# One 512-column matmul for the high and low halves of the input in the transposed up tiles

## The reference, cut to what matters

```python
D_MODEL = 1024; SEQ = 256; DEPTH = 2; D_FF = 2816; FFN_KERNEL = 3

def conv_ffn(h, w_up, conv_w, conv_b, w_down):
    u = causal_depthwise_conv(h @ w_up, conv_w, conv_b)
    gate, val = u[..., :D_FF], u[..., D_FF:]
    return (jax.nn.gelu(gate, approximate=True) * val) @ w_down
...
        y = conv_ffn(rms_norm(h, ffn_norm_pre[l]), ffn_w_up[l], ffn_conv_w[l], ffn_conv_b[l], ffn_w_down[l])
        h = h + rms_norm(y, ffn_norm_post[l])
```

## Time and profile before

| | us |
|---|---|
| median of 3 runs | 845.71 (845.55 to 846.62) |
| the profiled execution | 845.01 |
| its span, first to last instruction | 843.0 |
| TensorE busy | 820.3 (97% of the span) |
| VectorE busy | 615.0 (73%) |
| ScalarE busy | 498.7 (59%) |

### The profile page before, as it was taken

The page is one execution under the profiler, slowest core; times in us unless marked ns, Lnnn a source line. Parts: engine busy times, 40 slices in busy tenths (PEclk is TensorE's granted clock), DMA queues, the critical chain, the costliest instruction groups (busy, mean ns, idle before and its releaser), DMA issues.

```text
span 843.0 us, 12986 instructions
## 1 busy us (share of the span) xinstructions
PE 820.3 (97%) x5152; PEld 732.6 (87%) x5152; DVE 615.0 (73%) x1080; ACT 498.7 (59%) x765; POOL 28.4 (3%) x53
## 2 busy tenths in 40 slices
PE   3999999999999999999999999999999999999997
PEld 2998898889889999998899889888988899999885
DVE  5689996575675887886577899848567488877653
ACT  4555977565656666564454578656566466666441
POOL 2000000010010000000020000001000000000000
PEclk9999999999999999999999999999999999999999
DMA  9655343574474466557647553455535526565651
GB/s 338 226 175 175 126 148 112 165 237 139 125 248 131 147 200 189 171 190 225 198 143 255 172 156 106 142 173 194 206 112 178 186 89 197 190 200 180 208 187 50
DMA packets 40363, 147.31 MB, mean 175 GB/s; under 512 B 4528, under 2 KB 4656, under 8 KB 40304
## 3 DMA queue, kind: packets, MB, share of 16 engines
q1 hardware_dynamic: 38144, 138.90, 51.1%
q0 software_dynamic: 2160, 7.59, 2.7%
HBM read 145.43 MB, written 1.05 MB: 174 GB/s over the span
## 4 chain that ended last, share of the span: by engine, by line
PE 89%; DVE 5%; ACT 2%; DMA 2%; issue 2%; POOL 0%; SPq 0%; DVEq 0%; POOLq 0%; ACTq 0%
PE acc L1383 7%; PE acc L1385 6%; PE acc L1384 6%; PE acc L1366 4%; PE acc L1368 4%; PE acc L1367 4%; PE acc L1423 4%; PE acc L1425 3%; PE acc L1424 3%; PE psAB L1366 3%; PE psAB L1367 3%; PE psAB L1368 3%; PE psCD L1383 3%; PE psCD L1385 3%; PE psCD L1384 3%; PE psCD L1334 3%
## 5 line engine op out<-in xcount | busy, mean ns | idle before, releaser
L832 DVE TENSOR_TENSOR wlo<-raw,whi 128x1024 fp32r<-128x1024 f32 x240 | 288.1, 1221 | 84.0 <-ACT whi L479 81.7
L479 ACT ACTIVATE whi<-raw 128x1024 fp32r<-128x1024 f32 x240 | 249.8, 1057 | 104.0 <-PE acc L1368 45.3
L1383 PE MATMUL acc<-xT_hi,whi 128*128 128x256 f32 x432 | 123.4, 286 | 1.5 <-DVE wlo L832 1.5
L1384 PE MATMUL acc<-xT_lo,whi 128*128 128x256 f32 x432 | 122.2, 283 | 0.0
L1385 PE MATMUL acc<-xT_hi,wlo 128*128 128x256 f32 x432 | 122.2, 283 | 0.0
L1383 PEld LDWEIGHTS acc<-xT_hi,whi 128*128 128x128 f32 x432 | 82.8, 192 | 4.7 <-issue 2.7
L1384 PEld LDWEIGHTS acc<-xT_lo,whi 128*128 128x128 f32 x432 | 82.8, 192 | 0.2
L1385 PEld LDWEIGHTS acc<-xT_hi,wlo 128*128 128x128 f32 x432 | 82.8, 192 | 0.0
L1383 PE MATMUL psCD<-xT_hi,whi 128*128 128x256 f32 x192 | 54.6, 285 | 0.0
L1385 PE MATMUL psCD<-xT_hi,wlo 128*128 128x256 f32 x192 | 54.3, 283 | 0.0
L1384 PE MATMUL psCD<-xT_lo,whi 128*128 128x256 f32 x192 | 54.3, 283 | 0.0
(11 more groups left out here) (275 smaller groups left out, 2017.4 us busy)
## 6 DMA issues: line engine op xcount, KB each, us to landing
raw<-stream_dram SPq DMA_DIRECT2D x256, 512.0 KB, 4.0
gpre<-gain_dram POOLq DMA_DIRECT2D x7, 512.0 KB, 5.7
gpost<-gain_dram POOLq DMA_DIRECT2D x6, 512.0 KB, 5.4
memn<-mem_dram SPq DMA_DIRECT2D x2, 512.0 KB, 5.9
h<-x_dram SPq DMA_DIRECT2D x1, 1024.0 KB, 12.4
out_dram<-h SPq DMA_DIRECT2D x2, 512.0 KB, 2.6
cst<-const_dram SPq DMA_DIRECT2D x1, 896.0 KB, 16.9
gpre<-gain_dram SPq DMA_DIRECT2D x1, 512.0 KB, 5.3
```

What stands on the lines that cost most here:

```text
L479: act.activation(home(g)[0], raw[:, s * GW:(s + 1) * GW], ACT.Copy).then_inc(w_hi.sem, 1)
L832: dve.tensor_tensor(lo, raw[:, cols], hi.bitcast(F32), ALU.subtract).then_inc(w_lo.sem, 1)
L1383: pe.matmul(dst, whi[:, cols], hi[:, toks], start=k == 0 and c % 2 == 0, stop=False)
L1384: pe.matmul(dst, whi[:, cols], lo[:, toks], start=False, stop=False)
```

## The change

The input's halves become one tensor `xT`, so that `xT_both[:, :, k, :]` is the high and the low half of block k, 512 columns in two pieces. `halves_product` takes the place of `transposed_product` for tiles 2 to 10: for each (k, c) one matmul moves both halves past the `whi` block (512 columns, one PSUM bank: `whi`·hi in its first half, `whi`·lo in its second), and one adds `wlo`·hi (256 columns) to the first half. A chunk so takes a whole bank and a tile 4 banks; two sets of 4 are used in turn, and a tile waits for the sum of the tile two before it.

The two halves of a bank are added outside TensorE. ScalarE copies the second halves to `ffu` (`up_low`, 2 instructions of 512 columns), VectorE adds the first halves to them there (`up_sum`, 2 instructions of 512 columns), and `gate` and `up_taps` of tiles 2 to 10 read `ffu` in SBUF instead of PSUM. In both engines' lists one split stands now between these and `gate` / `up_taps`, and one after.

```diff
-        xT_hi = sb("xT_hi", KC * SEQ, F32R)
-        xT_lo = sb("xT_lo", KC * SEQ, F32R)
+        xT = sb("xT", 2 * KC * SEQ, F32R)
+        xT_hi, xT_lo = xT[:, 0:KC * SEQ], xT[:, KC * SEQ:2 * KC * SEQ]
+        xT_both = xT[:, :].rearrange("p (s k n) -> p s k n", s=2, k=KC)
...
+        ffu = V[:, D:D + 4 * SEQ]
...
-        up_banks = [psAB, accs[1], psCD, accs[0]]
+        up_banks = [psAB, [a[:, :] for a in accs[0]]]
 
         def up_chunk(j, c):
 
-            return up_banks[j % 4][c // 2][:, c % 2 * SEQ:(c % 2 + 1) * SEQ]
+            if j < 2:
+                return up_banks[j][c // 2][:, c % 2 * SEQ:(c % 2 + 1) * SEQ]
+            return ffu[:, c * SEQ:(c + 1) * SEQ]
...
+        def up_pair(j, n):
+
+            return ((psC, acc2[1]) if j % 2 == 0 else (psA, acc2[0]))[n]
...
                     if j >= 2:
-                        act.wait_ge(w_used.sem, w_used.at(l, G_UP + (j + 1) * PER_TILE))
+                        act.wait_ge(u_sum.sem, u_sum.at(l, j - 1))
...
+                def up_low(j):
+
+                    act.wait_ge(w_used.sem, w_used.at(l, G_UP + (j + 1) * PER_TILE))
+                    if j > 2:
+                        act.wait_ge(y_conv.sem, y_conv.at(l, j))
+                    for n in range(2):
+                        act.activation(ffu[:, n * 2 * SEQ:(n + 1) * 2 * SEQ].rearrange("p (c n) -> p c n", c=2),
+                                       up_pair(j, n)[:, :, SEQ:2 * SEQ], ACT.Copy).then_inc(u_lo.sem, 1)
...
                     split(G_UP + (j + 1) * PER_TILE - 1 + AHEAD)
+                    up_low(j)
+                    split(G_UP + (j + 1) * PER_TILE + AHEAD)
                     gate(j)
...
+                def up_sum(j):
+
+                    for n in range(2):
+                        dve.wait_ge(u_lo.sem, u_lo.at(l, 2 * (j - 2) + n + 1))
+                        lo = ffu[:, n * 2 * SEQ:(n + 1) * 2 * SEQ].rearrange("p (c n) -> p c n", c=2)
+                        e = dve.tensor_tensor(lo, up_pair(j, n)[:, :, 0:SEQ], lo, ALU.add)
+                    e.then_inc(u_sum.sem, 1)
...
                     split(G_UP + (j + 1) * PER_TILE - 1 + AHEAD)
+                    up_sum(j)
+                    split(G_UP + (j + 1) * PER_TILE + AHEAD)
                     up_taps(j)
...
+                                both = dst.rearrange("p (s n) -> p s n", s=2)
+                                if k == KC - 1:
+                                    pe.matmul(dst[:, 0:SEQ], wlo[:, cols], xT_both[:, 0, k, :], start=False, stop=False)
+                                    e = pe.matmul(both, whi[:, cols], xT_both[:, :, k, :], start=False, stop=True)
+                                else:
+                                    pe.matmul(both, whi[:, cols], xT_both[:, :, k, :], start=k == 0, stop=False)
+                                    e = pe.matmul(dst[:, 0:SEQ], wlo[:, cols], xT_both[:, 0, k, :], start=False, stop=False)
...
-                transposed_product(G_UP + 2 * PER_TILE + 1, 3, X, up_banks[2], k0=2)
-                for j in range(3, UP_TILES):
-                    if j >= 4:
-                        pe.wait_ge(y_conv.sem, y_conv.at(l, j - 3))
-                    transposed_product(G_UP + j * PER_TILE, PER_TILE, X, up_banks[j % 4])
+                halves_product(2, 1, 3)
+                pe.wait_ge(y_conv.sem, y_conv.at(l, 2))
+                halves_product(3)
+                for j in range(4, UP_TILES):
+                    pe.wait_ge(u_sum.sem, u_sum.at(l, j - 3))
+                    halves_product(j)
```

More of the change, by code:

```diff
@@ L226, in hybrid_trunk @@
         ffg = [V[:, b * 2 * SEQ:(b + 1) * 2 * SEQ] for b in range(2)]
-        def bank(name):
-            return ctx.enter_context(nc.psum_tensor(name, [P, NT], F32))
-        accs = [[bank(f"acc{s}{t}") for t in range(TOK)] for s in range(2)]
+        ffu = V[:, D:D + 4 * SEQ]
+        acc2 = [ctx.enter_context(nc.psum_tensor(f"acc{s}", [P, TOK, NT], F32)) for s in range(2)]
+        accs = [[a[:, t] for t in range(TOK)] for a in acc2]
         psA = ctx.enter_context(nc.psum_tensor("psAB", [P, 2, NT], F32))
@@ L235, in hybrid_trunk, with up_halves @@
         psCD = [psC[:, 0], psC[:, 1]]
-        up_banks = [psAB, accs[1], psCD, accs[0]]
+        up_banks = [psAB, [a[:, :] for a in accs[0]]]
         def up_chunk(j, c):
-            return up_banks[j % 4][c // 2][:, c % 2 * SEQ:(c % 2 + 1) * SEQ]
+            if j < 2:
+                return up_banks[j][c // 2][:, c % 2 * SEQ:(c % 2 + 1) * SEQ]
+            return ffu[:, c * SEQ:(c + 1) * SEQ]
+        def up_halves(j, n):
+            return up_pair(j, n // 2)[:, n % 2]
+        def up_pair(j, n):
+            return ((psC, acc2[1]) if j % 2 == 0 else (psA, acc2[0]))[n]
         attended = accs[1][1][:, 0:SEQ]
@@ L346, in hybrid_trunk @@
         u_tr = signal("u_tr", 2)
+        u_lo = signal("u_lo", 2 * (UP_TILES - 2))
+        u_sum = signal("u_sum", UP_TILES - 2)
         y_tap2 = signal("y_tap2", UP_TILES)
@@ L1386, in transposed_product, with halves_product @@
                                               stop=k == KC - 1 and c % 2 == 1)
+                        e.then_inc(w_used.sem, 1)
+                def halves_product(j, first=0, groups=PER_TILE):
+                    for g in range(G_UP + j * PER_TILE + first, G_UP + j * PER_TILE + first + groups):
+                        s = g % RING
+                        pe.wait_ge(w_lo.sem, w_lo.at(l, g + 1))
+                        for u in range(UNITS):
+                            k = (g - G_UP - j * PER_TILE) * UNITS + u
+                            for c in range(4):
+                                cols = slice(s * GW + u * NT + c * P, s * GW + u * NT + (c + 1) * P)
+                                dst = up_halves(j, c)
+                                both = dst.rearrange("p (s n) -> p s n", s=2)
[5 more added lines that the diff above has]
+                                    e = pe.matmul(dst[:, 0:SEQ], wlo[:, cols], xT_both[:, 0, k, :], start=False, stop=False)
                         e.then_inc(w_used.sem, 1)
@@ L1733, in up_flip @@
                 def up_flip(j):
+                    pe.wait_ge(rows_in.sem, rows_in.at(l, (j + 2) * TOK))
                     for t in range(TOK):
-                        pe.wait_ge(rows_in.sem, rows_in.at(l, (j + 1) * TOK + t + 1))
                         for c in range(4):
@@ L1751, in _ @@
                 up_flip(0)
-                transposed_product(G_UP + 2 * PER_TILE, 1, X, up_banks[2])
+                halves_product(2, 0, 1)
                 up_flip(1)
-                transposed_product(G_UP + 2 * PER_TILE + 1, 3, X, up_banks[2], k0=2)
-                for j in range(3, UP_TILES):
-                    if j >= 4:
-                        pe.wait_ge(y_conv.sem, y_conv.at(l, j - 3))
-                    transposed_product(G_UP + j * PER_TILE, PER_TILE, X, up_banks[j % 4])
+                halves_product(2, 1, 3)
[4 more added lines that the diff above has]
+                    halves_product(j)
                 G = tuple(gT[:, part * 2 * SEQ:] for part in range(2))
                 g_order = [4 * (k // 2) + k % 2 for k in range(FFC)]
-                pe.wait_ge(y_conv.sem, y_conv.at(l, UP_TILES - 2))
+                pe.wait_ge(u_sum.sem, u_sum.at(l, UP_TILES - 3))
                 for g in range(DOWN_GROUPS):
```

## The result

The changed kernel takes 863.44 us in the median (863.01 to 863.60), the kernel before beside it 845.63 (845.39 to 846.62). The ratio is 1.0206, with a 95% interval from 1.0194 to 1.0219: 2.1% slower. The prediction was 863.1.

What follows compares the result with a forecast made beforehand. The VectorE-ScalarE loop of 12.45 us a tile was to replace TensorE as the bound, delaying each layer by 8.7 us: 845.0 + 17.4 = 862.4, plus 0.7 to the median, 863.1 us; range 853 to 870.

Steps and rivals of the forecast that it cites:

- The bound changes: Tiles 2 to 10: the VectorE-ScalarE loop, 12.45 us, replaces TensorE, 11.09 us a tile, as what sets the pace.
- The loop: Waits between VectorE and ScalarE from one tile's taps to the next: 10.62 us before, 12.45 us after the change.
- adds and signal: Loop piece: two VectorE adds of 512 columns, 1.22 us, plus 0.12 us for the signal and ScalarE's start.
- gate until taps: Loop piece from the gate's start on ScalarE to the taps on VectorE: 1.94 us before, 2.11 us after.
- The 0.17 us for a gate that reads SBUF: Extra time for a gate's four ScalarE instructions reading SBUF instead of PSUM; the other bound was 0.
- Start and end: Stage edges: taps of tile 2 at 282.8, tile 10 12.1 us late, seventh down group 8.7 us late per layer.
- The step from the profiled execution to the median: Median of the runs taken as 0.7 us above the profiled execution: 862.4 becomes 863.1.
- The rival of the taps on SBUF: VectorE's taps get faster reading SBUF, 0.065 us each: loop 11.93 us, time 854 us; chance 0.12.
- the wide matmul's pace: TensorE's 512-column matmul in two pieces starts 0.227 us before the next; a pair takes 0.347 us.
- the change's own gain: TensorE's shorter matmul work: 0.43 us less a tile, 7.7 us for 18 tiles.
- The faster rival: TensorE stays the bound if the loop takes less than 11.09 us: 839 us; chance 0.06.
- tile 3's wait: In the faster rival's sum, 1.3 us a layer added for TensorE's wait at tile 3 for the taps of tile 1.

Runs made afterwards that it cites:

- n1_narrow: Changed kernel with three matmuls of 256 columns again per block and chunk, copies, adds and order kept: 863.63 us, ratio 1.0220 to the kernel before.
- n2_no_adds: Changed kernel without the new copies and adds, so the input's low half is missing from tiles 2 to 10: 842.37 us, ratio 0.9968.
- n3_one_add: Changed kernel without the first of each tile's two adds, copies and waits kept: 852.89 us, ratio 1.0092 to the kernel before.
- n8_sum_earlier: Changed kernel with the adds one weight split earlier in VectorE's list alone: 850.86 us, ratio 1.0055 to the kernel before.
- n9_no_split_between: Changed kernel with copies and adds straight before gate and taps, splits back where they stood before the change: 886.83 us, ratio 1.0477.
- n4_reorder: Changed kernel's same instructions in another order on ScalarE and VectorE, nothing left out: 842.21 us, ratio 0.9965 to the kernel before.

## Why the prediction was right

**The bound changes.** It rested on reading the spare time of the other two engines from the loop, 10.62 us where TensorE did not hold it, and not from VectorE's 73%. n1_narrow and n2_no_adds show it from both sides: with TensorE's part undone nothing moves, with the adds out everything comes back.

**The loop.** The sum was 12.45 us, measured are 12.47. Piece by piece from the round shown above, in the order of the prediction: taps 3.29 (3.26 predicted), split 1.14 (1.135), multiply 0.72 (0.71), high half 0.53 (0.54), first copy until the split 1.08 (1.08), two splits 2.28 (2.27), adds and signal 1.31 (1.34), gate until taps 2.12 (2.11). The 0.17 us for a gate that reads SBUF, taken from the four instructions of L643, was there: the gate's four take 1.99 us (306.13 until the next instruction of ScalarE at 308.12) where they took 1.79 (288.63 until 290.42, the next line there):

```profile
290.42 2.01 ACT L479 ACTIVATE whi<-raw 128x1024 fp32r<-128x1024 f32 x2
```

n3_one_add, n8_sum_earlier and n9_no_split_between are three more sums of the same kind, 11.87, 11.67 and 13.63 us, and 11.85, 11.66 and 13.59 came.

**Start and end.** The profiled execution of the changed kernel is 0.6 us late before the stage begins (its taps of tile 0 start at 265.43, those of before at 264.81). With that taken off, the taps of tile 2 start at 282.69 (282.8 predicted), those of tile 10 at 382.42 (382.4), the sixth down group at 390.56 (390.4), the seventh at 393.36 (393.1). In the kernel before, the seventh starts at 384.44:

```profile
384.44 0.39 PE L1366 MATMUL psAB<-whi,gT 128*128 128x512 f32 x1
```

That is 8.9 us a layer. The span grew by 18.5 us, 17.9 without the 0.6; the sum had 17.4.

**How near the number is, is in part luck.** For the profiled execution the sum gives 862.4, and 863.48 was measured, 1.1 us more: 0.5 us in the two stages and the 0.6 us before them, which no term had. The step from the profiled execution to the median, 0.7 us, was taken from the kernel before; in the changed kernel the profiled execution is no faster than the median. The two misses cancel to 0.3 us.

**The rival of the taps on SBUF** fell: eight of them take 3.29 us from SBUF and took 3.26 from PSUM. The Trainium skill's table (VectorE: DVE Perf Modes, The TRN2 errata), by which SBUF as a source is 62 cycles cheaper than PSUM, is not borne out by these rows.

**What was mis-sized** is a term that did not matter to the time: the wide matmul's pace. I took 0.227 us from matmuls of 512 columns elsewhere. A pair of 0.347 is found in parts of the stage, but 0.353 in others, and where TensorE held the taps in n2_no_adds a tile took 11.28 instead of 11.09. So TensorE waits 1.2 us a tile and not 1.3 to 1.4, in two pauses of 0.5 to 0.65 us from start to start and not 0.6 to 0.8, and the change's own gain, once freed, is 3 to 4 us and not 7.7. The faster rival's 839 would therefore not have come about even with a short loop; n4_reorder shows what does, 842.2. (The 1.3 us that this rival had for tile 3's wait came from no row; the trace after has 1.24 at 276.54.) The saving of a pair, 7 to 13 ns, is over the 2.5 ns that follow from the formula of the Trainium skill (TensorE: Matmul & The Clock Gate, Back-to-back issue gap). That section gives the formula for the gap of an isolated matmul, and not for a stream in which each has its own weight load, as here, so it was never a rule against this gain. TensorE's busy share was predicted at 93 to 95% and is 96%: a matmul's record runs on while the next is already streaming (records of 0.40 us start 0.24 us apart), so short pauses vanish partly in it. The chain is the better witness.

## What to carry to other kernels

Where engines work to and fro in a fixed order, read the loop from a stretch in which the bounding engine does not hold it; that figure, and not the busy share, is the slack which new work may use. Before moving work off the busiest engine, add the pieces from one step to its next occurrence; every instruction that stands between two waits counts in full. And then look for the places where the helper waits: the same instructions cost 21 us in one order and nothing in another.
